# Spreading eight bias transfers, reordering the vector engine's attention work, and moving row scaling and clearing between engines

## The reference

```python
# first block
iscore = einsum('bqh,bqhs->bqs', wib, relu(dots)); _, idx = lax.top_k(iscore, topk)   # topk = 64
q_b    = einsum('bsr,rhd->bshd', c_q, w_uq);  v_b = einsum('bsr,rhd->bshd', c_kv, w_uv)
p      = softmax(where(causal, sc, -inf));    o = einsum('bhqs,bshd->bqhd', p, v)      # 8 heads
merged = sigmoid(g_a) * y_a + sigmoid(g_b) * y_b
h      = rmsnorm(h, norm_final_g)             # output rows of the first block, input of the second
# second block, MoBA layer
bias_own = rel_table[t5_bucket(dist_own)]; s_own = q @ k * scale + bias_own
q, k, v  = split(rmsnorm(h, norm_mix) @ w_in, 3)
```

## Time and profile before

| what | value |
|---|---|
| median of 3 runs | 1011.52 us (1010.19 to 1012.46) |
| the profiled execution: its time, its span | 1011.16 us, 1009.3 us |
| PE busy | 984.7 us, 98% of the span |
| DVE busy | 681.3 us, 68% |
| ACT busy | 542.8 us, 54% |
| POOL busy | 44.8 us, 4% |
| mean clock granted to PE | 0.996 of full speed |

### The profile page before, as it was taken

The page is one execution under the profiler, slowest core; times in us unless marked ns, Lnnn a source line. Parts: engine busy times, 40 slices in busy tenths (PEclk is TensorE's granted clock), DMA queues, the critical chain, the costliest instruction groups (busy, mean ns, idle before and its releaser), DMA issues.

```text
span 1009.3 us, 15668 instructions
## 1 busy us (share of the span) xinstructions
PE 984.7 (98%) x6348; PEld 842.5 (83%) x6348; DVE 681.3 (68%) x853; ACT 542.8 (54%) x708; POOL 44.8 (4%) x68
## 2 busy tenths in 40 slices
PE   7999999999999999999998999999999999999997
PEld 6887667898888888887887888888899898888885
DVE  5688787688777787777665555556655566555564
ACT  6676564566556565634445444444545555444452
POOL 1220000000000005000020000000000000000000
PEclk9999999999999999999999999999999999999999
DMA  9364244567565545844348656555544346556551
GB/s 307 97 207 148 87 130 146 167 205 233 177 197 188 187 161 161 262 147 155 123 139 233 207 175 206 173 203 179 180 164 166 120 158 224 189 185 199 176 165 42
DMA packets 121283, 175.89 MB, mean 174 GB/s; under 512 B 3167, under 2 KB 89770, under 8 KB 121226
## 3 DMA queue, kind: packets, MB, share of 16 engines
q1 hardware_dynamic: 118860, 168.82, 50.9%
q0 software_dynamic: 1600, 5.09, 2.0%
q10 hardware_dynamic: 766, 1.16, 0.5%
HBM read 173.82 MB, written 1.25 MB: 173 GB/s over the span
## 4 chain that ended last, share of the span: by engine, by line
PE 70%; issue 19%; DVE 6%; ACT 2%; DMA 2%; POOL 1%; SPq 0%; POOLq 0%; ACTq 0%; DVEq 0%
PE ps L1842 20%; PE ps L1892 16%; PE ps L1863 10%; PE ps L1891 7%; PE ps L1879 5%; PE ps L1906 2%; DVE w_lo L1085 1%; DMA raw<-in_ffn_w 1%; PE ps L1914 1%; PE ps L2329 1%; PE ps L1894 1%; PE ps L1957 1%; PE ps L2392 1%; PE ps L1988 1%; DMA raw<-in_w_in 1%
## 5 line engine op out<-in xcount | busy, mean ns | idle before, releaser
L1085 DVE TENSOR_TENSOR w_lo<-raw,w_hi 128x2048 fp32r<-128x2048 f32 (+3 forms) x156 | 352.3, 2262 | 129.1 <-ACT w_hi L543 128.7
L1892 PE MATMUL ps<-x_both,w_hi 128*128 128x512 f32 x992 | 342.7, 396 | 0.0
L543 ACT ACTIVATE w_hi<-raw 128x2048 fp32r<-128x2048 f32 (+3 forms) x161 | 302.3, 1879 | 63.5 <-PE ps L1842 40.1
L1891 PE MATMUL ps<-x_both,w_lo 128*128 128x256 f32 x868 | 242.0, 279 | 0.0
L1892 PEld LDWEIGHTS ps<-x_both,w_hi 128*128 128x128 f32 x992 | 179.1, 188 | 34.5
L1891 PEld LDWEIGHTS ps<-x_both,w_lo 128*128 128x128 f32 x868 | 163.6, 189 | 5.5
L798 ACT ACTIVATE work<-ps 128x512 f32<-128x512 f32 x66 | 39.3, 596 | 150.4 <-PE ps L1892 134.6
L1842 PE MATMUL ps<-w_hi,x_both 128*128 128x512 f32 (+1 forms) x320 | 101.5, 387 | 0.1
L1842 PE MATMUL ps<-w_hi,hid_hi 128*128 128x512 f32 x240 | 94.7, 394 | 3.8 <-DVE work L1489 3.3
L1842 PE MATMUL ps<-w_lo,hid_hi 128*128 128x512 f32 x240 | 93.9, 391 | 0.0
L1842 PE MATMUL ps<-w_hi,hid_lo 128*128 128x512 f32 x240 | 93.9, 391 | 0.0
(11 more groups left out here) (295 smaller groups left out, 1273.0 us busy)
## 6 DMA issues: line engine op xcount, KB each, us to landing
raw<-in_ffn_w SPq DMA_DIRECT2D x66, 1024.0 KB, 5.1
raw<-in_w_up SPq DMA_DIRECT2D x22, 1024.0 KB, 5.1
raw<-in_hgrn_w_in SPq DMA_DIRECT2D x16, 1024.0 KB, 5.5
raw<-in_w_in SPq DMA_DIRECT2D x12, 1024.0 KB, 5.1
raw<-in_moba_w_in SPq DMA_DIRECT2D x12, 1024.0 KB, 5.2
raw<-in_w_down SPq DMA_DIRECT2D x11, 1024.0 KB, 5.0
raw<-in_w_out SPq DMA_DIRECT2D x4, 1024.0 KB, 5.2
raw<-in_hgrn_w_out SPq DMA_DIRECT2D x4, 1024.0 KB, 5.0
```

Of the source, the lines that this page charges most:

```text
L543: act.activation(w_hi[:, n % RING, 0:kc * cols], raw[:, n % RING, 0:kc * cols], ACT.Copy).then_inc(s["hi_ready"], 1)
L1085: dve.tensor_tensor(w_lo[:, n % RING, sl], raw[:, n % RING, sl], f32(w_hi[:, n % RING, sl]), ALU.subtract).then_inc(s["lo_ready"], 1)
L1891: pe.matmul(out[:, 0, :], w_lo[:, n % RING, at], x_hi[:, k, :], start=False, stop=False)
L1892: ins = pe.matmul(out, w_hi[:, n % RING, at], x_both[:, k, :, :], start=(k == 0), stop=(k == DC - 1))
```

## The change

There are seven edits.

1. The eight bias DMAs no longer go out together; each waits on POOL for three more products of `ffn1`.
2. POOL clears `near` and `pairs` right after issuing a gain broadcast at the start of the first feed-forward part, and the scaling of `h` goes from POOL to ACT.
3. `uv` and `uq` change banks, so `uv` waits for a copy that frees banks 6 and 7, `uq` for the last two relus; ACT copies the values first, then the keys.
4. Ahead of the units, DVE splits granule 10 before three pieces of `add_heads`, and rotates the queries (L1258) before a round of `largest`.
5. In the units each step of DVE is either `after(u)`, between the probabilities of `u` and the maxima of `u+1`, or `hidden(u)`, after these maxima, while ACT takes exponentials. `latent_lo` works one unit later than before and sits in `after`, `largest` mostly too, and the splitting is nearly all in halves in `hidden`.
6. Unit 6's mask is added by PE.
7. In the MoBA layer's first product, the four products with `x_hi` of a half come first and wait for ACT's rounding, then the four with `x_lo`, which wait for DVE.

```diff
-MASKED_BY_DVE = range(6, 16)
+MASKED_BY_DVE = range(7, 16)
@@ POOL
             gain(3, a["norm_mix_2"][0])
+            pool.memset(near.rearrange("p a b -> p (a b)"), 0.0)
+            pool.memset(pairs.rearrange("p a b c -> p (a b c)"), 0.0).then_inc(s["pairs_zero"], 1)
...
-            for t in range(TT):
-                pool.wait_ge(s["rstd_ready"], 7 + t)
-                pool.wait_ge(s["scaled_done"], 2 * t + 2)
-                pool.wait_ge(s["ssq_ready"], 6 + 2 * t)
-                pool.tensor_tensor(h[:, t, :], scaled[:, t, :], rstd[:, 4 + t:5 + t].broadcast_to((P, D)), ALU.mult).then_inc(s["h_final"], 1)
-            pool.memset(near.rearrange("p a b -> p (a b)"), 0.0)
-            pool.memset(pairs.rearrange("p a b c -> p (a b c)"), 0.0).then_inc(s["pairs_zero"], 1)
...
             for r in range(0, P, COPIES):
+                pool.wait_ge(s["products_done"], G["ffn1"] + 3 + 3 * (r // COPIES))
                 pool.dma_start(bias[r:r + COPIES], skew).then_inc(s["bias_in"], 16)
@@ ACT
-            act.wait_ge(s["products_done"], G["uk"] + 1)
+            act.wait_ge(s["products_done"], G["uv"] + 1)
+            act.activation(v_b, ps[:, 6:8, :], ACT.Copy).then_inc(s["v_copied"], 1)
...
+            for t in range(TT):
+                act.wait_ge(s["rstd_ready"], 7 + t)
+                act.activation(h[:, t, :], scaled[:, t, :], ACT.Copy, scale=rstd[:, 4 + t:5 + t]).then_inc(s["h_final"], 1)
@@ DVE
-            lo_of(8, 9)
-            for n in range(4, 6):
-                add_heads(n)
-            lo(10)
-            for n in range(6, 8):
+            lo_of(8, 9, 10)
+            for n in range(4, 7):
                 add_heads(n)
             lo(11)
+            add_heads(7)
...
-            ROUNDS = {0: 1, 1: 1, 3: 1, 4: 1}
+            ROUNDS = (0, 1, 2, 4)
...
+            def after1(u):
+                if 2 <= u <= 9:
+                    latent_lo(u - 2)
+                if u in ROUNDS:
+                    largest()
+                if u == 3:
+                    lo_half(g0 + 2, 1)
+                if u == 5:
+                    choose_keys()
                 if u == 14:
+                    gate_branch_b(0)
+                    output_lo1(12)
+                if u == 15:
...
+                    output_lo1(13)
+            def hidden1(u):
+                if u == 0:
+                    largest()
+                elif u == 1:
+                    lo(g0 + 1)
+                elif u == 2:
+                    lo_half(g0 + 2, 0)
+                elif u in (3, 4):
+                    lo_half(g0 + 3, u - 3)
+                elif u < 15:
+                    lo_half(g0 + 4 + (u - 5) // 2, (u - 5) % 2)
+                bounds(u)
+            units(0, 16, hidden1, after1)
+            output_lo1(14)
+            lo(ba + 1)
+            gate_branch_b(1)
             output_lo1(15)
@@ PE
-            pe.wait_ge(s["relu_done"], 7)
+            pe.wait_ge(s["proj_copied"], 4)
...
+                pe.wait_ge(s["relu_done"], 7 + t)
...
-            pe.wait_ge(s["qb_copied"], 1)
+            pe.wait_ge(s["v_copied"], 1)
             token_product(G["gate0"], 0, 6, True, False)
...
-                    for k in range(4):
-                        ready(t, 4 * g + k)
-                        for x in (x_hi, x_lo):
+                    for x, ready in ((x_hi, "half_hi"), (x_lo, "half_lo")):
+                        pe.wait_ge(s[ready], step(6, t, g))
+                        for k in range(4):
```

More of the change, by code:

```diff
@@ L1327, in _ @@
             lo(g0)
-            ROUNDS = {0: 1, 1: 1, 3: 1, 4: 1}
-            assert 4 + sum(ROUNDS.values()) == TOPK // 8
+            ROUNDS = (0, 1, 2, 4)
+            assert 4 + len(ROUNDS) == TOPK // 8
             def maxima(u):
@@ L1354, in maxima, with units @@
                 dve.tensor_scalar(neg_max[:, c:c + 2], rowmax[:, c:c + 2], -scale, None, ALU.mult).then_inc(s["neg_ready"], 1)
-            def units(first, count, extra, between=None):
+            def units(first, count, hidden, after):
                 if first == 0:
@@ L1371, in units @@
                     ins.then_inc(s["prob_ready"], 1)
-                    if between:
-                        between(u)
-                    if u == 0:
-                        largest()
-                    if u == TOPK // 8 - 3:
-                        choose_keys()
+                    after(u)
                     if u + 1 < first + count:
                         maxima(u + 1)
-                    for _ in range(ROUNDS.get(u, 0)):
-                        largest()
-                    extra(u)
+                    hidden(u)
             def lo_half(n, half):
@@ L1427, in bounds @@
                     then(dve.tensor_scalar(lb_rest, lb, -1.0, 1.0, ALU.mult, ALU.add))
-            def fill_lo(u):
-                bounds(u)
-                if 1 <= u <= 8:
-                    latent_lo(u - 1)
+            ba = G["branch_a"]
+            def after1(u):
[7 more added lines that the diff above has]
+                    choose_keys()
                 if u == 14:
+                    gate_branch_b(0)
+                    output_lo1(12)
+                if u == 15:
                     dve.wait_ge(s["ohi_ready"], 1)
                     dve.tensor_tensor(x_lo[:, 0:2, :], o_T[:, 0:2, :], f32(x_hi[:, 0:2, :]), ALU.subtract).then_inc(s["olo_ready"], 1)
-                if u >= 13:
-                    output_lo1(u - 1)
-                if u in (1, 2):
-                    lo(g0 + u)
-                elif u in (5, 7, 9, 11):
-                    lo_half(g0 + 2 + u // 2, 0)
-                elif u % 2 == 1:
-                    lo(g0 + 2 + u // 2)
-                elif u in (6, 8, 10, 12):
-                    lo_half(g0 + 1 + u // 2, 1)
-                if u == 15:
-                    gate_branch_b(1)
-            units(0, 16, fill_lo, lambda u: gate_branch_b(0) if u == 14 else None)
+                    output_lo1(13)
+            def hidden1(u):
+                if u == 0:
+                    largest()
+                elif u == 1:
[11 more added lines that the diff above has]
+            gate_branch_b(1)
             output_lo1(15)
-            ba = G["branch_a"]
             def gate_branch_a(c, t):
@@ L1759, in output_lo, with hidden2 @@
                                   f32(hi_part[:, 2 * j:2 * j + 2, dst]), ALU.subtract).then_inc(s["mo_lo"], 1)
-            def fill_lo2(u):
+            def hidden2(u):
                 if u > 16:
                     output_lo(u - 1)
-            units(16, 8, fill_lo2, lambda u: lo(nm + u - 9))
+            units(16, 8, hidden2, lambda u: lo(nm + u - 9))
             lo(nm + 15)
@@ L2081, in _ @@
                         for q, (x, w) in enumerate(hid_parts):
-                            ins = pe.matmul(ps[:, 6 - 2 * t + half, 0:384], x[:, k, P * t:P * t + P],
+                            ins = pe.matmul(ps[:, 2 + 2 * t + half, 0:384], x[:, k, P * t:P * t + P],
                                             w[:, n % RING, 768 * k + 384 * half:768 * k + 384 * half + 384],
@@ L2381, in qk_product @@
                 feature_product(nm + QK[i], 6 + i % 2)
-            ready = operand_ready(6)
             def values_high(t):
```

15 lines of the change are left out of this document (5 added, 10 removed).

## The result

The changed kernel takes 1001.04 us (median of 4 runs, 1000.87 to 1001.67), the kernel before took 1010.86 us beside it (4 runs, 1009.24 to 1012.46): a ratio of 0.9904, 95% interval 0.9886 to 0.9922. The forecast was 1000.7. The profiled execution took 1000.87 us, its span is 999.0. One execution among those of the experiments, of the run that undoes the MoBA edit, took 1388 us at a granted clock of 0.66 and is left out of its median.

The account below looks back on a forecast made before the run. PE was taken as the bound, busy nearly all the span. Gains of 4.3 + 0.4 + 5.0 + 0.85 = 10.55 us from 1011.16 gave 1000.6; forecast 1000.7 us, range 998.8 to 1002.6, chance 0.70.

Parts of the forecast that it names:

- Units: First attention's units: PE's waits for probabilities and gating go, PE sets the pace; gain 4.3 us, bounds 2.8 to 4.7.
- ten waits at 0.09 us: In the units, each wait of PE costs about 0.09 us beyond its idle time; ten give 0.9 us.
- The 0.1 us expected to be lost in unit 1: Unit 1, the fullest: DVE needs 5.5 us between two probabilities against PE's 5.0; 0.1 us counted lost.
- Start of `ffn1`: Without the bias burst, PE's 3.3 us stall and 1.74 us of slow products go: 5.0 us, bounds 3.3 to 5.3.
- The slack behind the granule: At the start of `ffn1`, DVE would finish 1.7 us before PE runs out of work.
- The price of 0.7 us for each transfer: In `ffn1`, each spread bias transfer delays one granule by 0.7 us, hidden by 7 us of slack.
- MoBA border: First MoBA product: PE can begin at 716.85 instead of 717.71 us; gain 0.85 us, bounds 0.5 to 1.07.
- Ahead of the units: Before the first attention's units: granule 11 is split near 64.3 instead of 64.6 us; gain 0.4, bounds -0.5 to 0.9.
- POOL and ACT: Scaling of `h` moved to ACT near 390 us, clearing moved to 201.5 us: quicker DVE gains nothing, 0 in all.
- The rival on clearing: Near 202 us, POOL's clearing holds DVE's operand split: 1.2 us less gain, 1001.9 us; chance 0.06.
- The two large terms: The units' 4.3 us and the 5.0 us at the start of `ffn1`.

Follow-up runs that it names:

- the traces of the experiment: The changed kernel with the old order of the sixteen units on DVE and unit 6's mask on DVE again: 1005.80 us.
- the two experiments: Changed kernel with the eight bias transfers in one burst again: 1006.06 us; kernel before with only their spread: 1006.64 us.
- the three bursts: Changed kernel with four, six or all eight bias transfers started together at the start of `ffn1`: 1000.77, 1001.45 and 1006.06 us.
- nothing by the experiment: Changed kernel with the old order ahead of the units (banks, ACT's copies, granule 10, rotation): 1001.02 us.
- 0 by the experiment: Changed kernel with the old order of the first MoBA product, and POOL's scaling of `h` and late clearing, restored: 1001.81 us.

## Why the prediction was right, and where it was not

**Units.** Forecast 4.3 us, won 4.32 by the leads from the first unit's transpose (+0.17) to branch A (-4.15), and 4.31 in the traces of the experiment, whose medians are 4.8 us apart. The sum counted ten waits at 0.09 us where the earlier trace rows has nine, which is 0.1 us. The pace is PE's from the start. The 0.1 us expected to be lost in unit 1 was not: its transpose follows the first by 5.07 us, and unit 2's follows by 5.05, with no wait. The wait near unit 14's values stayed, as forecast (L2165 in the list of waits, 0.3 us).

**Start of `ffn1`.** Forecast 3.3 + 1.74 = 5.0 us, won 5.06, and 5.0 and 4.6 us by the two experiments. The slack behind the granule is 1.45 us, I had worked out 1.7. The granule landed 4.84 us after its issue. The spread cost nothing, as forecast: its transfers landed in 3.1 to 5.7 us, and ACT waited for no load. The price of 0.7 us for each transfer, from dividing the lateness by nine, lies between the 0.57 and 0.81 us of the three bursts; it is no constant. It was not used in the sum. The 0.75 of the earlier trace rows, which I read as a clock between the two levels, is an average: in the kernel before, too, the clock was 0.50 for 3.4 us, from 547.5 to 550.9 us, and 1.00 after it. The 1.74 us taken from the products' times was right all the same. Of the Trainium skill's rule that the engines take turns between queues (DMA: Bandwidth & Descriptors, Queues, rings and completion order), the runs bear out that a transfer shares with the granule in flight; how the share grows with the number they don't explain.

**MoBA border.** Forecast 0.85 us, won 0.72. PE begins 0.74 us after ACT's first rounding starts (706.67 to 707.41); I had taken 0.6.

**Ahead of the units: the step that failed.** I forecast that granule 11 would be split by 64.3 us, since DVE would be through with granule 10 earlier, and counted 0.4 us. Measured: 0.1 us (a lead of +0.27 us at ACT's copy of the input projection's block, +0.17 at the first unit), and nothing by the experiment. The part between the products did come true: this wait of the kernel before, at `uv`, is gone,

```profile
PE ps L2071 <- ACT work L656: 0.4, 1, 0.4
```

and from the start of `uv` to that of `uq` are 1.51 us instead of 1.75. Timelines of ACT, DVE and PE in the changed kernel:

```profile
58.98 0.60 ACT L651 ACTIVATE work<-ps 128x512 f32<-128x512 f32 x1 [1.05 <-DVE work L1283]
60.20 0.60 ACT L651 ACTIVATE work<-ps 128x512 f32<-128x512 f32 x1 [0.61 <-DVE work L1283]
```
```profile
62.70 2.29 DVE L1084 TENSOR_TENSOR w_lo<-raw,w_hi 128x2048 fp32r<-128x2048 f32 x1 [1.53 <-ACT w_hi L538]
```
```profile
65.14 0.47 PE L1847 MATMUL ps<-w_hi,x_both 128*128 128x512 f32 x1 [0.96 <-DVE w_lo L1084]
```

I had the two relus later by the 0.8 us of DVE's pieces, and took granule 11's rounding to be done all the same by the time DVE was free. But the relus wait for those pieces one after the other, 1.05 and 0.61 us, the rounding stands behind both, and DVE then waits 1.53 us for it. The 0.7 us that PE saved ahead of `uv` and between `uv` and `uq` it stood at the gate product, where it waits 0.96 us. The cause is shown by the run in which the rounding passes relu 7: the wait at the gate product is gone.

**POOL and ACT.** Forecast 0, and 0 by the experiment, once the border's 0.73 us is taken from its 0.77, as far as a median can tell. DVE's splits are quicker near 390 us and nobody waits for them; ACT's scaling lies in its wait for PE:

```profile
387.11 2.19 ACT L911 ACTIVATE h<-work,stat 128x1024 f32<-128x1024 f32 x2
391.63 0.60 ACT L918 ACTIVATE work<-ps 128x512 f32<-128x512 f32 x1 [2.34 <-PE ps L1919]
```

The rival on clearing did not come. Timelines of DVE and POOL at the border to the first feed-forward part:

```profile
197.46 1.29 DVE L1103 SCALAR_TENSOR_TENSOR x_both<-ps,x_both 128x512 fp32r<-128x512 f32 x2 [0.92 <-ACT x_both L554]
198.66 4.48 DVE L1084 TENSOR_TENSOR w_lo<-raw,w_hi 128x2048 fp32r<-128x2048 f32 x2
...
197.41 0.55 POOL L492 MEMSET work<- 128x512 f32 x1
197.87 1.82 POOL L493 MEMSET work<- 128x2048 f32 x1
```

DVE's operand splits take 1.29 us for two and the granules 4.48 us for two, as at the same place in the kernel before (201.52 and 202.73 us) and at the MoBA border (707.30 and 708.50 us), where POOL does nothing beside them. The clearing ends at 199.7 us, so 1.0 us of it lies beside the first granule's splitting. The Trainium skill (GPSIMD Engine Reference, Specifications) has contention where VectorE has two SBUF inputs, and names there no condition on GpSimd's side. For clearing the traces show none; for POOL's two-input work they agree, 5.97 us against 4.48.

**What nobody forecast.** 0.48 us of the lead came at one gap of PE, which the profile puts down to its own issuing: 1.60 us before, 1.12 after. It is no gain of the change. In the second profile of the very same program it was 0.77 us, and from 1.1 to 1.6 in the others. What sets it stays open.

The sum was 10.55 us of gain from the profiled execution's 1011.16, and 10.29 came (1000.87). The 0.3 us missing ahead of the units, 0.13 at the MoBA border, 0.1 that went between branch A and 387 us, and the 0.27 us by which the changed kernel's trace begins later come to 0.8 us; the 0.48 us of that gap and the 0.1 more at `ffn1` offset most of them. The two large terms, 9.3 of the 10.55 us, were right in mechanism and size. That the total is right to 0.3 us is partly luck: without the gap it would be 9.8 us. The experiments add up to 10.5 us (5.0, 4.8, 0 and 0.77), where the medians are 9.8 apart, which their intervals allow.

## What to carry to other kernels

A burst of small transfers is dear only where it meets the one large load that has little slack: move it to where the loads have time in hand before thinning it out. In a pipeline of several engines, ask of each instruction that waits what stands in front of it to fill the wait; an order works as a whole, and one step put back can cost more than all of them. A mean clock between the two levels is an average over the window: narrow the window before reading it. Before counting a step as earlier, follow the engine between: the rounding that DVE needed stood on ACT behind two relus that needed DVE.

## What the runs showed of the hardware that was not expected

- A load of 1 MB with transfers of 128 KB on another queue started just ahead of it took 4.8 us to land with none of them, 7.1 with four, 8.4 with six and 11.3 with eight. In the kernel before, in the window from 530 to 535 us, the DMA engines were busy throughout (share 1.03) and moved only 155 GB/s; in the changed kernel it was 265 GB/s at a share of 0.79.
- After stalls of PE of 3.33, 2.94 and 2.55 us the granted clock was 0.50 for 3.4 us and then 1.00 again, and the first two cost 1.7 us each in the 24 products behind them. In the third the clock fell only 1.4 us after PE had gone on. After a delay of 0.2 us it stayed at 1.00.
- Clearing 128x2048 elements on POOL did not slow DVE's two-input splitting in the 1.0 us in which it lay beside it; POOL's own two-input operation did, by 1.5 us for the 1.6 us that it lay beside (to 389.72 us, from 388.11).
- Two profiles of one program differ by 0.35 us in a gap of PE with no instruction of another engine behind it, so a difference of that size in one place is not the change's.
